# The q and k projections of layer 1 turned by VectorE block transposes and an HBM bounce instead of on TensorE

## The reference

```python
qkv = (h @ sb_w_qkv[j]).reshape(b, s, 3, C_HEADS, C_HEAD_DIM)     # h = rms_norm(x, w)
# per block of 128 queries:
z = jnp.einsum('bqhd,bkhd->bhqk', qf[:, q0:q1], kf[:, :q1])        # qf = q * C_HEAD_DIM ** -0.5
mask = (q0 + jnp.arange(SB_QBLOCK))[:, None] > jnp.arange(q1)[None, :]
log_beta = jax.nn.log_sigmoid(z)
log_keep = jnp.where(mask, jax.nn.log_sigmoid(-z), 0.0)
later = lax.cumsum(log_keep, axis=3, reverse=True) - log_keep
w = jnp.where(mask, jnp.exp(log_beta + later), 0.0)
outs.append(jnp.einsum('bhqk,bkhd->bqhd', w, vf[:, :q1]))
```

## Time and profile before

| | |
|---|---|
| median of 3 executions | 2122.1 us |
| the profiled execution, its own time | 2121.32 us |
| span of its instructions | 2119.5 us |
| TensorE, granted clock over the span | 9 tenths or more in every slice (1.00 for the core) |
| VectorE busy | 1230.3 us, 58% |
| ScalarE busy | 972.6 us, 46% |
| GpSimd busy | 112.2 us, 5% |
| weight traffic and the rest, mean | 205 GB/s |

### The profile page before, as it was taken

The page is one execution under the profiler, slowest core; times in us unless marked ns, Lnnn a source line. Parts: engine busy times, 40 slices in busy tenths (PEclk is TensorE's granted clock), DMA queues, the critical chain, the costliest instruction groups (busy, mean ns, idle before and its releaser), DMA issues.

```text
span 2119.5 us, 22740 instructions
## 1 busy us (share of the span) xinstructions
PE 2105.6 (99%) x9436; PEld 1738.7 (82%) x9436; DVE 1230.3 (58%) x1366; ACT 972.6 (46%) x1122; POOL 112.2 (5%) x189
## 2 busy tenths in 40 slices
PE   9999999999999999999999999999999999999999
PEld 7877878888888888888788888878888888888887
DVE  6777555555455555556566466565555455555554
ACT  6566454444444443445455445454443444434443
POOL 1000110010001000011000000110000001000010
PEclk9999999999999999999999999999999999999999
DMA  9544776675666756677655555676675666656673
GB/s 320 190 138 152 227 223 225 204 236 196 198 208 218 229 193 192 211 232 240 215 164 161 179 161 172 220 232 210 215 239 183 196 217 224 213 198 198 206 234 135
DMA packets 210503, 434.85 MB, mean 205 GB/s; under 512 B 9233, under 2 KB 9249, under 8 KB 210145
## 3 DMA queue, kind: packets, MB, share of 16 engines
q1 hardware_dynamic: 197600, 392.72, 55.8%
q0 software_dynamic: 12384, 38.56, 7.0%
q10 hardware_dynamic: 416, 2.13, 0.3%
HBM read 413.45 MB, written 19.92 MB: 204 GB/s over the span
## 4 chain that ended last, share of the span: by engine, by line
PE 88%; DMA 6%; DVE 2%; issue 1%; ACT 1%; POOL 1%; SPq 0%; POOLq 0%; ACTq 0%
PE acc L1021 28%; PE acc L1023 28%; PE acc L1022 28%; DMA spread<-blocks 3%; DMA blocks<-folded 2%; POOL spread L428 1%; DVE w_lo L683 1%; PE turn L1037 1%; DVE xT_lo L743 1%; ACT xT_hi L497 1%; DMA raw<-in_w_in 1%; DVE folded L732 1%; PE turn L1101 1%; PE turn L1147 0%; PE zb L1122 0%
## 5 line engine op out<-in xcount | busy, mean ns | idle before, releaser
L683 DVE TENSOR_TENSOR w_lo<-raw,w_hi 128x1024 fp32r<-128x1024 f32 x744 | 899.6, 1221 | 583.9 <-ACT w_hi L478 583.4
L478 ACT ACTIVATE w_hi<-raw 128x1024 fp32r<-128x1024 f32 x744 | 783.1, 1058 | 888.1 <-PE acc L1023 885.6
L1021 PE MATMUL acc<-w_hi,xT_hi 128*128 128x512 f32 x2016 | 793.0, 393 | 7.5 <-DVE w_lo L683 7.4
L1023 PE MATMUL acc<-w_hi,xT_lo 128*128 128x512 f32 x2016 | 785.8, 390 | 0.0
L1022 PE MATMUL acc<-w_lo,xT_hi 128*128 128x512 f32 x2016 | 785.7, 390 | 0.0
L1021 PEld LDWEIGHTS acc<-w_hi,xT_hi 128*128 128x128 f32 x2016 | 378.8, 188 | 90.6 <-issue 9.1
L1023 PEld LDWEIGHTS acc<-w_hi,xT_lo 128*128 128x128 f32 x2016 | 378.6, 188 | 78.9
L1022 PEld LDWEIGHTS acc<-w_lo,xT_hi 128*128 128x128 f32 x2016 | 378.9, 188 | 78.3 <-issue 1.7
L1021 PE MATMUL acc<-w_hi,m_hi 128*128 128x512 f32 x960 | 374.8, 390 | 1.2 <-DVE w_lo L683 1.2
L1023 PE MATMUL acc<-w_hi,m_lo 128*128 128x512 f32 x960 | 373.9, 389 | 0.0
L1022 PE MATMUL acc<-w_lo,m_hi 128*128 128x512 f32 x960 | 373.9, 389 | 0.0
(11 more groups left out here) (137 smaller groups left out, 577.9 us busy)
## 6 DMA issues: line engine op xcount, KB each, us to landing
raw<-in_w_gate SPq DMA_DIRECT2D x88, 1024.0 KB, 5.2
raw<-in_w_up SPq DMA_DIRECT2D x88, 1024.0 KB, 5.8
raw<-in_w_down SPq DMA_DIRECT2D x88, 1024.0 KB, 5.1
raw<-in_w_qkv SPq DMA_DIRECT2D x48, 1024.0 KB, 5.2
raw<-in_w_out SPq DMA_DIRECT2D x32, 1024.0 KB, 5.1
raw<-in_w_in SPq DMA_DIRECT2D x26, 1024.0 KB, 5.1
blocks<-folded POOLq DMA_DIRECT2D x34, 512.0 KB, 4.0
spread<-blocks POOLq DMA_DIRECT2D x136, 128.0 KB, 6.2
```

Of the source, the lines that this page charges most:

```text
L478: nc.scalar.activation(w_hi[:, h.slot, :, :], raw[:, h.raw_slot, 2 * h.part:2 * h.part + 2, :], ACTF.Copy).then_inc(hi_ready, 1)
L683: nc.vector.tensor_tensor(w_lo[:, h.slot, :, :], raw[:, h.raw_slot, 2 * h.part:2 * h.part + 2, :], f32(w_hi[:, h.slot, :, :]), ALU.subtrac ...
L1021: nc.tensor.matmul(dst, xh, wh, start=h.opens and k == 0, stop=False)
L1023: ins = nc.tensor.matmul(dst, xl, wh, start=False, stop=h.closes and k == 1)
```

## The change

- The 8 chunks of q and k (4 groups x 2) are no longer turned by TensorE. Each is folded on VectorE and sent through the bounce, so there are 42 bounces in place of 34. q and k get a buffer each (`qk1[:, 0]`, `qk1[:, 1]`).
- The fold of q stands at the step at which q ends, that of k at the step at which k ends, and in the first group 2 steps later: q 14 and k 18 there, q 8 and k 16 in the others.
- q is not copied: TensorE reads it as the moving operand right out of `spread`, in runs of 32 values. k is copied by ScalarE from `spread` into `kT1` one step before z, with `k1_copied` as the signal; TensorE waits for it. GpSimd may reuse a slot of `spread` once z of that group is made.
- z stands at step `z_at` = fold of k + 6, that is 24 in the first group and 22 in the others, in place of 18; all that follows moves with it, so that the last step of the attention is 35 or 33 in place of 29.
- The bookkeeping of folds and turns is renumbered (`splits`, `FOLDS`, `turns`).

```diff
+Z_LAG = 6
     def fold_at(self, c):
-        return self.ends[c] + (2 if self.paired and c == 1 and self.ph.renews else 0)
+        return self.ends[c] + (2 if self.paired and c == 1 and self.ph.name != "up" else 0)
+    def z_at(self):
+        return self.fold_at(1) + Z_LAG
...
-            qk1 = sb("qk1", [P, TT, CH], F32, c3)
+            qk1 = sb("qk1", [P, 2, TT, CH], F32, c3)
-            qT1 = sb("qT1", [P, GRP, SEQ], F32, c3)
...
                 if F >= 2:
-                    pool.wait_ge(fold_lo, F - 1)
+                    split, g = FOLDS[F - 2]
+                    if split:
+                        pool.wait_ge(fold_lo, splits(F - 2) + 1)
+                    else:
+                        pool.wait_ge(z_done, 2 * g + 2)
...
             def qkv_work(it, t):      # ScalarE
                 ph, g = it.ph, it.i
-                if t == it.ends[0] + 1:
-                    take_hi(ph.turn(g, 0), [qT1[:, 0:2, :].rearrange("p h t -> p (h t)")], [turn[:, 0:CH]])
-                if t == it.ends[1] + 1:
-                    take_hi(ph.turn(g, 1), [kT1[:, 0:2, :].rearrange("p h t -> p (h t)")], [turn[:, 0:CH]])
+                zt = it.z_at()
+                if t == zt - 1:
+                    F = ph.fold(2 * g + 1)
+                    act.wait_ge(fold_landed, 16 * QUARTERS * (F + 1))
+                    nc.scalar.activation(by_tile(kT1[:, :, :]), spread_tiles(F), ACTF.Copy).then_inc(k1_copied, 1)
...
             def qkv_work(it, t):      # VectorE
-                if t == it.ends[0] + 1:
-                    take(ph.turn(g, 0), qT1[:, 2:4, :].rearrange("p h t -> p (h t)"), turn[:, CH:2 * CH])
-                if t == it.ends[1] + 1:
-                    take(ph.turn(g, 1), kT1[:, 2:4, :].rearrange("p h t -> p (h t)"), turn[:, CH:2 * CH])
+                for c in range(2):
+                    if t == it.fold_at(c):
+                        dve.wait_ge(acc_read, 2 * ph.chunk(g, c) + 2)
+                        fold(ph.fold(2 * g + c), qk1[:, c])
...
             def qkv_work(it, t):      # TensorE
-                for c in range(2):
-                    if t == it.ends[c] + 1:
-                        pe.wait_ge(acc_read, 2 * ph.chunk(g, c) + 2)
-                        turn_chunk(ph.turn(g, c), qk1)
+                zt = it.z_at()
                 for p in range(2):
                     n = 2 * g + p
-                    if t == 18 + p:
-                        pe.wait_ge(act_took, ph.turn(g, 1) + 1)
-                        pe.wait_ge(dve_took, ph.turn(g, 1) + 1)
+                    if t == zt + p:
+                        pe.wait_ge(k1_copied, g + 1)
...
                         for h in range(2):
-                            kh, qh = kT1[:, 2 * p + h, :], qT1[:, 2 * p + h, :]
+                            kh = kT1[:, 2 * p + h, :]
+                            qh = spread[:, ph.fold(2 * g) % 2, :, :, (2 * p + h) * BLK:(2 * p + h + 1) * BLK]
```

More of the change, by code:

```diff
@@ L118, in __init__ @@
         self.before, self.rows0, self.up0, self.read0, self.turn0, self.fold0 = sums
-        self.turns = {"in": 23, "qkv": 4}.get(self.name, 0)
-        self.folds = self.count if self.name == "up" else self.chunks if self.renews else 0
+        self.turns = {"in": 23, "qkv": 2}.get(self.name, 0)
+        self.folds = {"up": 1, "qkv": 2}[self.name] * self.count if self.name in ("up", "qkv") else self.chunks if self.renews else 0
         self.iterations = []
@@ L151, with splits @@
 CHUNKS = [(it, c) for it in ITERATIONS for c in range(it.ph.chunks)]
-FOLDS = [(it, 1, it.i) if it.ph.name == "up" else (it, c, c) for it in ITERATIONS if it.ph.folds
-         for c in ([1] if it.ph.name == "up" else range(it.ph.chunks))]
+FOLDS = [(it.ph.name != "qkv", it.i) for it in ITERATIONS if it.ph.folds
+         for c in ([1] if it.ph.name == "up" else range(2) if it.ph.name == "qkv" else range(it.ph.chunks))]
+def splits(F):
+    return sum(split for split, _ in FOLDS[:F])
 def running(g):
@@ L327, in build @@
         masks_rounded = sem("masks_rounded")
+        k1_copied = sem("k1_copied")
         w_exp, w_ready = sem("w_exp"), sem("w_ready")
@@ L736, in fold_take_lo @@
             def fold_take_lo(F, dst, src, hi, scale=None):
-                dve.wait_ge(fold_hi, F + 1)
+                dve.wait_ge(fold_hi, splits(F) + 1)
                 for n, (d, s, h) in enumerate(zip(dst, src, hi)):
@@ L762, in leave @@
                     if c == 0:
-                        evacuate(it, c, qk1, C_DIM ** -0.5)
+                        evacuate(it, c, qk1[:, 0], C_DIM ** -0.5)
                     else:
-                        evacuate(it, c, (qk1, v1)[c - 1])
+                        evacuate(it, c, (qk1[:, 1], v1)[c - 1])
                 elif ph.name == "up":
@@ L958, in qkv_work @@
                         ins.then_inc(w_ready, 1)
-                    if t == 26 + 3 * p:
+                    if t == zt + 8 + 3 * p:
                         at = (slice(None), slice(4 * g + 2 * p, 4 * g + 2 * p + 2), slice(None))
-                        take_lo(ph.turn(g, 2 + p), [m_lo[at]], [turn[:, 0:CH].rearrange("p (h t) -> p h t", h=2)], [m_hi[at]])
+                        take_lo(ph.turn(g, p), [m_lo[at]], [turn[:, 0:CH].rearrange("p (h t) -> p h t", h=2)], [m_hi[at]])
             def between(it, t):
@@ L1001, in stationary_ready @@
                 elif prev.name == "qkv":
-                    pe.wait_ge(dve_took, prev.turn(h.k0 // 4, 2 + h.k0 // 2 % 2) + 1)
+                    pe.wait_ge(dve_took, prev.turn(h.k0 // 4, h.k0 // 2 % 2) + 1)
                 elif prev.folds:
-                    pe.wait_ge(fold_lo, prev.fold(h.k0 // 4) + 1)
+                    pe.wait_ge(fold_lo, splits(prev.fold(h.k0 // 4)) + 1)
             def half(it, h):
@@ L1120, in qkv_work @@
                         for h in range(2):
-                            kh, qh = kT1[:, 2 * p + h, :], qT1[:, 2 * p + h, :]
-                            nc.tensor.matmul(zb[:, h * CH:h * CH + SEQ], kh[:, 0:P], qh[:, :], start=True, stop=True)
-                            ins = nc.tensor.matmul(zb[:, h * CH + SEQ:h * CH + SEQ + P], kh[:, P:], qh[:, P:], start=True, stop=True)
+                            kh = kT1[:, 2 * p + h, :]
+                            qh = spread[:, ph.fold(2 * g) % 2, :, :, (2 * p + h) * BLK:(2 * p + h + 1) * BLK]
+                            nc.tensor.matmul(zb[:, h * CH:h * CH + SEQ].rearrange("p (t a b) -> p t a b", t=TT, a=QUARTERS),
+                                             kh[:, 0:P], qh, start=True, stop=True)
+                            ins = nc.tensor.matmul(zb[:, h * CH + SEQ:h * CH + SEQ + P].rearrange("p (a b) -> p a b", a=QUARTERS),
+                                                   kh[:, P:], qh[:, 1], start=True, stop=True)
                         ins.then_inc(z_done, 1)
-                    if t == 23 + 3 * p:
+                    if t == zt + 5 + 3 * p:
                         if g == 0:
@@ L1139, in qkv_work @@
                         ins.then_inc(sum_done, 1)
-                    if t == 26 + 3 * p:
+                    if t == zt + 8 + 3 * p:
                         pe.wait_ge(w_ready, n + 1)
                         pe.wait_ge(acc_read, 2 * ph.chunk(g, 2) + 2)
-                        turn_free(ph.turn(g, 2 + p))
+                        turn_free(ph.turn(g, p))
                         for h in range(2):
```

25 lines of the change are left out of this document (13 added, 12 removed).

## The result

The changed kernel takes 2127.2 us (median of 13, 2123.6 to 2131.9) against 2120.1 us of the kernel before, timed beside it (13 runs, 2117.3 to 2126.5). The ratio is 1.0029, with a 95% interval of 1.0022 to 1.0036. That is 6.1 us slower; the two medians lie 7.1 us apart. The forecast was 2123.0 us against 2122.1, 0.9 us slower, in a range of 2117 to 2129.5. The time fell inside, but in its upper part, and the growth was several times the 0.9 us: a term was missing.

A forecast was written before the change was run, and what follows sets the result against it. TensorE's own work was taken to bound qkv; 8.3 us off (7.2 + 1.1) and 9.2 us on (5.0 + 3.6 + 0.6) gave net +0.9 us, so 2123.0 us against 2122.1, with a range of 2117 to 2129.5 us.

The forecast's parts named there:

- What bounds the kernel: In qkv TensorE, busy 239.97 of 240 us, sets the end; time taken from it or waited by it counts in full.
- The transposes: On TensorE in qkv: 64 transposes removed in 8 batches, 0.90 us a batch, 7.2 us off.
- The waits at z: TensorE waiting for k: 5.0 us for three later groups, weight loads included, and 3.6 us in the first group.
- I take no second cost there: At TensorE's wait for k1_copied in the first group: nothing added beyond the wait, as ScalarE's split is made in time.
- rival 2: Bounces land later than in up, TensorE waits on k1_copied; 2130.2 us with two such groups; chance 0.15.
- The shift: Attention steps moved in qkv: v's evacuations clear p = 0's weights, -1.1 us; p = 1's weights meet q's evacuation, +0.6 us.
- The sum: Whole kernel: 8.3 us off and 9.2 us on, net +0.9 us.
- (1) no wait: At z: the bounce is in time and the transposes are pure gain, -8.3 + 0.6, so 2114.4 us; chance 0.11.
- the prediction's estimate by that page: In k's bounce: reads with their issues take about 4 us, write 3.2 us, bounce over some 5 us earlier.
- (3) z's reads of q in runs of 32: TensorE reads q slowly in z: at most 15.7 us more, 2138.7 us; at half that 2130.9; chance 0.04.
- (4): On TensorE in qkv: transposes ran in gaps, so their removal freed no time; 2130.2 us; chance 0.01.

## Why the prediction was right, and where it was not

- **What bounds the kernel** held: every term appears in full in TensorE's schedule of the stretch.
- **The transposes**, 7.2 us: measured 7.23 us.
- **The waits at z**, 5.0 + 3.6 us: 9.4 us of gaps in the changed kernel's trace, 8.4 in the second. By group 4.7, 0.6, 2.9 and 1.2 us against 3.6 and 1.65 three times. The rows of the up phase carried over: from fold to copy the three later bounces of k took 13.8, 16.1 and 14.4 us, in the span of the 22 (13.8 to 18.2 us). First and longest, as said.
- **"I take no second cost there"** is the step that failed. It was said of the work behind the waiting instruction, and ScalarE and VectorE did keep up; but TensorE's clock falls behind a wait, 4.1 us in the stretch of this trace and 1.6 us in the out phase (1.8 us in the stretch of the kernel's second trace, 9.3 with all four waits long). The prediction said that the clock stays at 1.00 and gave no reason. In its rows the longest wait for w_lo was 2.3 us, with a clock of 1.00 over the whole span. Those rows could not speak for a wait of 3.6 us, and this cost belonged in the sum or in rival 2. The Trainium skill, page "TensorE: Matmul & The Clock Gate", section "The HAM clock gate (the "warmup" mystery)", has the default as the slow state, and activity as what lifts it; the trace agrees, 0.50 behind the waits of 5.9 to 6.6 us and 1.00 with the same waits filled.
- **The shift**, -1.1 + 0.6 us: measured -0.74 together, and the weight load's waits went from 4 to 2.
- **The sum**, +0.9 us: by the trace +5.8 us in the stretch, of which the clock is 4.1; 3.0 us more came behind the stretch, at the renewal in the out phase, to which the prediction gave nothing. That the time still fell inside the range is partly luck. The range is 12.5 us wide for a growth of 0.9, and the kernel before measured 2120.1 us this time, 2.0 us below the median that the forecast started from.
- **The rivals.** (1) no wait: false as placed, but it is what the kernel becomes with z later, and its net gain of 7.7 us was met (8.4 in the stretch, 7.6 in the time). The rule of the Trainium skill, page "DMA: Bandwidth & Descriptors", section "Anatomy of one DMA — SWDGE (gpsimd) path", by which the bounce would be in time, does not hold here: the trace does not agree, as from the first read's issue to the copy k's four bounces took 7.7 to 10.0 us, where the prediction's estimate by that page was about 4. (2) later bounces: the waits were about as forecast and did not decide it. (3) z's reads of q in runs of 32: 1.22 us from z's start to the next weight matmul, before and after, where the clock is 1.00, so no cost. (4) false, by the transposes put back.

## What to carry to other kernels

On an engine that is busy for 99%, moving work off it only pays if what replaces it is scheduled by its measured latency, the queue in front of it included; here one to three steps of slack turned 6 us lost into 7.6 us gained. Price a wait of TensorE as its length plus, perhaps, the slow matmuls behind it: here 1.5 to 2.8 us from waits of 1.9 us on, though not behind every one. Sum with the long end where two transfers share a queue. Steps written out by hand collide with the next iteration's evacuations: recount them after every shift.

## What the runs showed of the hardware

The clock fell to 0.50 behind waits of 2.20 and 2.65 us (in the out phase), 2.74, 2.88, 4.51 and 5.9 to 6.6 us. It stayed at 1.00 behind waits of 1.7, 2.3 and once 3.25 us, so a wait of the same length went either way. Three traces show a fall behind a shorter wait, ahead of the changed part: 1.89 us with z at 22 and 20, and 1.93 us both in the second trace with z at 26 and 24 and in the kernel with the first group's wait filled. The last, below, had a wait of 2.01 us later on that left the clock at 1.00. So the expectation for z at 25 and 23, that its wait of 1.7 us would be too short for a fall, came true, but the 2.3 us that it gives as harmless is no limit.

```profile
1012.67 0.47 PE L1039 MATMUL acc<-w_hi,xT_hi 128*128 128x512 f32 x1 [1.93 <-DVE w_lo L700]
...
1013.70:1017.20 3.50, 3.50 (x10) 2.73 (x9) 1.91 (x7) 2.30 (x4) 0.96 (x2) 0.51 1.01 312
```

Each fall in qkv cost 1.7 to 2.8 us beyond the wait, the two in the out phase 1.5 and 1.6 us. Matmuls on constants kept the clock up at no cost but their own time: none where they ended ahead of k, some 0.9 us where they ran on past it.
